# Three of eight token tiles through dense expert products, beside the gather of the other five

## The reference

```
xn = rms_norm(h, norm_mix)                       # keys and branches stages
merged = sum over 3 branches of sigmoid(gate_b) * (y_b @ w_proj_b)
h = h + merged @ w_out                           # merge
xt = rms_norm(h, norm_ffn)
q = (xt @ wq).reshape(T, 8, 2, 128);  s = einsum('thpc,hpkc->thpk', q, keys)
s1, i1 = top_k(s[:, :, 0], 16);  s2, i2 = top_k(s[:, :, 1], 16)
top_s, sel = top_k(all 256 sums s1 + s2, 16);  eid = i1 * 128 + i2 of the selected
gate = softmax(top_s)
act = gelu(u_tab[eid] . xt);  h = h + sum of gate * act * v_tab[eid]   # 8 heads x 16
h = h + sigmoid(rms_norm(h, norm_ple) @ ple_gate) * (p @ ple_proj)
```

## Time and profile before

| | |
|---|---|
| median of 3 runs | 4248.98 us (4239.84 to 4253.56) |
| profiled execution, its own time | 4245.94 us |
| its span | 4244.1 us, 36303 instructions |
| TensorE busy | 3058.3 us, 72% |
| VectorE busy | 2838.0 us, 67% |
| ScalarE busy | 1270.4 us, 30% |
| GpSimd busy | 1201.3 us, 28% |
| DMA | 1206.54 MB, mean 284 GB/s; 1073.81 MB of it by GpSimd's queue |
| mean granted TensorE clock | 0.845 |

### The profile page before, as it was taken

The page is one execution under the profiler, slowest core; times in us unless marked ns, Lnnn a source line. Parts: engine busy times, 40 slices in busy tenths (PEclk is TensorE's granted clock), DMA queues, the critical chain, the costliest instruction groups (busy, mean ns, idle before and its releaser), DMA issues.

```text
span 4244.1 us, 36303 instructions
## 1 busy us (share of the span) xinstructions
PE 3058.3 (72%) x7816; PEld 1457.8 (34%) x7816; DVE 2838.0 (67%) x5382; ACT 1270.4 (30%) x3456; POOL 1201.3 (28%) x1092
## 2 busy tenths in 40 slices
PE   8979998899999556665666656566667666566655
PEld 4535555444444323232232223223323233232321
DVE  3345555111111498889888888888888888888885
ACT  3223333010111133343333333333333333333322
POOL 0000000000000144444444444444443444444442
PEclk9989998899999778797787788778777877787877
DMA  4330010610110699999999999999999999999996
GB/s 169 115 112 32 30 41 28 240 42 27 40 42 27 264 411 395 414 398 403 381 377 401 398 375 405 384 381 407 390 409 368 409 394 377 406 394 397 410 403 275
DMA packets 192741, 1206.54 MB, mean 284 GB/s; under 512 B 21232, under 2 KB 27632, under 8 KB 60912
## 3 DMA queue, kind: packets, MB, share of 16 engines
q0 software_dynamic: 147456, 1073.81, 62.2%
q1 hardware_dynamic: 42864, 123.25, 8.0%
q10 hardware_dynamic: 2304, 8.39, 0.5%
HBM read 1173.91 MB, written 31.46 MB: 284 GB/s over the span
## 4 chain that ended last, share of the span: by engine, by line
DVE 27%; DMA 14%; issue 14%; PE 5%; ACT 3%; DVEq 1%; POOL 1%; ACTq 0%; POOLq 0%
DMA e_rows<-in_peer_uv,e_at 14%; DVE e_acc L1346 8%; DVE e_prod L1336 7%; PE e_acc L1110 2%; PE e_p_q L117 2%; DVE e_top_at L1298 2%; DVE e_best_at L1298 1%; DVE e_top L1297 1%; DVE e_best L1297 1%; DVE e_s L1300 1%; PE e_p_t L1124 1%; DVE e_hot L1324 1%; DVE e_expert L1325 1%; DVE e_cand L1300 1%; POOL e_rows L1030 1%
## 5 line engine op out<-in xcount | busy, mean ns | idle before, releaser
L1110 PE MATMUL e_acc<-e_rows,e_diag 128*128 128x512 f32 x2048 | 1318.8, 783 | 974.2 <-ACT e_diag L1247 973.8
L1030 POOL DMA_INDIRECT e_rows<-in_peer_uv,e_at x1024 | 1172.9, 1145 | 1556.6 <-DVE e_acc L1346 1216.4
L1336 DVE SCALAR_TENSOR_TENSOR e_prod<-e_rows,e_xn 128x1024 bf16<-128x1024 f32 x1024 | 1223.6, 1223 | 257.2 <-DMA e_rows<-in_peer_uv,e_at 166.0
L1110 PEld LDWEIGHTS e_acc<-e_rows,e_diag 128*128 128x128 f32 x2048 | 444.1, 236 | 1729.9 <-ACT e_diag L1247 1346.2
L1346 DVE SCALAR_TENSOR_TENSOR e_acc<-e_rows,e_wts,e_acc 128x1024 f32<-128x1024 f32 x504 | 647.8, 1285 | 56.3 <-ACT e_wts L1248 56.2
L1024 POOL CAST e_at<-e_expert 128x16 uint32 (+1 forms) x64 | 28.2, 441 | 1439.6 <-DVE e_expert L1325 1439.3
L1243 ACT ACTIVATE e_dots<-e_dots 128x2 f32<-128x2 f32 x512 | 104.1, 203 | 1017.3 <-DVE e_prod L1336 995.3
L117 PE MATMUL e_p_q<-e_wq,e_xnt 128*128 128x256 f32 (+1 forms) x1024 | 271.3, 425 | 25.5 <-ACT e_xnt L1177 19.0
L117 PE MATMUL m_p_g<-m_wg,m_xnt 128*128 128x512 f32 x640 | 281.2, 592 | 0.0
L117 PEld LDWEIGHTS e_p_q<-e_wq,e_xnt 128*128 128x128 f32 x1024 | 228.4, 224 | 110.6 <-issue 67.1
L937 DVE TENSOR_TENSOR m_part<-m_p_p,m_sg 128x512 f32<-128x512 f32 x32 | 22.4, 700 | 299.3 <-PE m_p_p L117 299.3
(11 more groups left out here) (250 smaller groups left out, 3073.8 us busy)
## 6 DMA issues: line engine op xcount, KB each, us to landing
e_rows<-in_peer_uv,e_at POOLq DMA_INDIRECT x1024, 9.0
m_wg<-in_w_gates SPq DMA_DIRECT2D x5, 2048.0 KB, 17.2
mix_w_branches<-in_w_branches_kept SPq DMA_DIRECT2D x8, 768.0 KB, 4.6
kept_yt<-b_yt SPq DMA_DIRECT2D x8, 768.0 KB, 3.6
m_yt<-kept_yt SPq DMA_DIRECT2D x8, 768.0 KB, 4.8
m_wp<-in_w_proj SPq DMA_DIRECT2D x6, 1024.0 KB, 16.3
e_wq<-in_peer_wq SPq DMA_DIRECT2D x1, 5120.0 KB, 24.9
k_x<-in_x SPq DMA_DIRECT2D x8, 512.0 KB, 5.5
```

The source lines that it names most:

```text
L1030: pool.indirect_dma_start(out=rows[:, n % SLOTS, :], out_offset=None, in_=A["peer_uv"], in_offset=bass.IndirectOffsetOnAxis(ap=at[:, b, n: ...
L1110: ins = pe.matmul(acc2[:, hs], diag[k % 2][:], rows[:, n % SLOTS, D + half * HB:D + (half + 1) * HB], start=first, stop=last)
L1336: dve.scalar_tensor_tensor(out=prod[n % 2][:], in0=rows[:, n % SLOTS, 0:D], scalar=1.0, in1=xn[:], op0=ALU.mult, op1=ALU.mult, accum_out=d ...
```

## The change

`merge_stage` and `experts_stage` become one `late_stage`, written out without loops in numbered slots by a planner (`Plan`). Tiles come in groups: 5, 6, 7, then 0, 1, then 2, 3, 4. Within a group each weight chunk of 1 MB (`CHUNK` = 2048 columns by 128 partitions) is loaded once into a ring of five (`RING`) and used by all the group's tiles; no weights are kept.

Tiles 5 to 7 (`DENSE`) gather nothing. All 16384 experts are computed for their 384 tokens: 32 blocks of 512 experts, each with four first products (`S`, eight matmuls 128x128 by 128x384, gelu on ScalarE, product with the gates on VectorE) and six second products (`V`, four matmuls of 512 columns, added to the sum by VectorE). The gates come from a DRAM tensor `g` of 16384 x 384 numbers: SP fills it with zeros in the keys stage (64 DMAs of 0.39 MB), and GpSimd scatters each chosen gate into it by indirect DMAs of 128 single numbers that add to what is there, 16 a head, 384 in all. Each head waits for the landing of the tile's last head. 192 of them are issued before the first gather, the other 192 two behind each gather of the first 48 slots.

The other five tiles are gathered, 640 gathers, in 320 slots of one pair each (`first` to `end`). Of four places VectorE now adds three and TensorE one (`on_tensor`); the sum `acc` lies in SBUF. The planner spreads the jobs of group 2, the dense blocks and the per-layer gate by their TensorE times evenly over these slots, behind the diagonal product of the slot before. Scores go over DRAM. Searches are done for 26 heads before the first pair, then one head in eight slots. The core of the diff (`sp` of the keys stage, the planner, and the programs of the slots):

```diff
+                for a in range(cleared.shape[2]):
+                    sp.dma_start(cleared[t][:, a, :], zeros[:]).then_inc(zeros_in, 16)
...
+GROUPS = ((5, 6, 7), (0, 1), (2, 3, 4))
...
+def on_tensor(n):
+    return n % 4 == 3
...
+            self.group(g)
+            if g == 1:
+                self.start = self.of["score", g, 3]
+        self.dense()
+        self.ple(DENSE + tuple(range(GATHER - 1)))
...
+                    for m in (2 * part, 2 * part + 1):
+                        self.add((i, m), "S", 5.3, pa=1, chunk=c, n_chunks=1, s=i, m=m)
...
+                    for d in range(len(DENSE)):
+                        self.add((i - 1, part, d), "V", 3.5, pb=1, chunk=c, n_chunks=1, s=i - 1, half=part, d=d)
...
+        self.first = slot + 3
+        rest = list(jobs)
+        us, budget = 0.0, sum(job.us for job in rest) / (PAIRS - 6)
...
+            slot = self.first + int(us / budget) + late
...
+            def load_chunk(n):
+                if n >= RING:
+                    before = plan.last_job[n - RING]
...
+                source, at = plan.chunks[n]
+                sp.dma_start(chunk(n), A[source][at]).then_inc(ring_in[n % RING], 16)
...
+                pool.wait_ge(chosen, q + 1)
+                pool.tensor_copy(at_dense[:, q, :], expert_of(q)).then_inc(dense_at_ready, 1)
...
+                wait(pool, gates_added[d], q // len(DENSE) * TOPK * 16)
...
+                pool.indirect_dma_start(out=X["g"], out_offset=bass.IndirectOffsetOnAxis(ap=at_dense[:, q, k:k + 1], axis=0),
+                                        in_=gates[:, q, k:k + 1], in_offset=None, compute_op=ALU.add).then_inc(gates_added[d], 16)
...
+            early = PH * len(DENSE) * TOPK - 8 * 24
...
+            for g in range(PAIRS):
+                row(2 * g)
+                for q, k in todo[done:done + SCATTERS_A_SLOT // 2]:
+                    scatter(q, k)
...
+            for s in range(plan.n_slots):
+                g = pair_of(s - 1)
+                if g is not None:
+                    for r in (2 * g, 2 * g + 1):
+                        if on_tensor(r % TOPK):
+                            weigh(r)
+                for job in plan.at[s]:
+                    programs[job.kind](job)
...
+                for job in plan.at[s - 1] if s else ():
+                    if job.kind in programs:
+                        programs[job.kind](job)
...
+                if pair_of(s) is not None:
+                    weights(pair_of(s))
...
+                for job in plan.at[s - 1] if s else ():
+                    if job.kind in programs:
+                        programs[job.kind](job)
+                g = pair_of(s - 1)
+                if g is not None:
+                    for r in (2 * g, 2 * g + 1):
+                        if not on_tensor(r % TOPK):
+                            weigh(r)
...
+                if pair_of(s) is not None:
+                    dot(2 * pair_of(s))
+                    dot(2 * pair_of(s) + 1)
+                for q, part in plan.parts[s]:
+                    (search_keys, search_pairs, choose)[part](q)
```

More of the change, by code:

```diff
@@ new lines, in weigh @@
+            def weigh(r):
+                c, n = divmod(r, TOPK)
+                pe.wait_ge(diag_ready, n_pe(r) + 1)
+                if r % NSEL < 4:
+                    wait(pe, h2_ready, r // NSEL)
+                first, last = r % NSEL < 4, r % NSEL >= NSEL - 4
+                for half in range(2):
+                    hs = slice(half * HB, (half + 1) * HB)
+                    ins = pe.matmul(acc2[:, hs], diag[n_pe(r) % 2][:], rows[:, r % SLOTS, D + half * HB:D + (half + 1) * HB], start=first, stop=last)
+                ins.then_inc(acc2_done, 1)
@@ new lines, in _ @@
+            qturn_of = {job.y: job for job in plan.jobs if job.kind == "qturn"}
+            programs = {"gate": sigmoid_gate, "turn": keep_merged, "xt": keep_normed, "query": keep_query, "qturn": keep_turned, "score": keep_scores,
+                        "S": activate, "hturn": keep_sum, "pgate": sigmoid_sum}
+            norms_at = [[] for _ in range(plan.n_slots)]
+            for g, group in enumerate(GROUPS):
+                for i in range(len(group)):
+                    norms_at[plan.of["out", g, 1, i].slot + 2].append((g, i))
@@ L1397, in _ @@
-            for r in range(LEAD):
-                order.turn()
-                search(r, 0)
-                search(r, 1)
-                pairs(r)
-                choose(r, part(r, 0, N))
-                reciprocal_sum(r)
-            tiles(dve, tile)
-            reciprocal_rms(T - 1)
-            output(T - 1)
-SPILLS = {"xnt": [T, P, DC * P], "v": [T, P, RW], "kt": [T, P, RW], "yt": [T, P, 3 * RW], "pp": [T, P, D], "h": [T, P, D], "xn": [T, P, D]}
+                to = expert_of(q)
+                ins = dve.tensor_reduce(to, hot[:].rearrange("p a k b -> p a (k b)"), AX.X, ALU.add)
@@ new lines, in finish @@
+            def finish(t):
+                dve.wait_ge(acc_done, n_dve((t + 1) * NSEL))
+                dve.wait_ge(acc2_done, n_pe((t + 1) * NSEL))
+                tt(acc[:, t % 2, :], acc[:, t % 2, :], acc2[:], ALU.add).then_inc(h2_ready, 1)
+                dve.wait_ge(h2_ready, t + 1)
+            programs = {"proj": merge, "out": add_input, "S": gate_block, "V": add_block, "hturn": reciprocal_rms, "pgate": output}
+            scales_at = [[] for _ in range(plan.n_slots)]
+            for g, group in enumerate(GROUPS):
+                for i in range(len(group)):
+                    scales_at[plan.of["out", g, 1, i].slot + 3].append((g, i))
```

1249 lines of the change are left out of this document (763 added, 486 removed).

## The result

The changed kernel takes 4346.47 us (median of four runs, 4342.12 to 4350.7), the one before 4250.49 us beside it: 1.0232 times as long, interval 1.0211 to 1.0253. It is 2.3% slower. Forecast were 3948 us; even the range, up to 4200, was missed. A difference of 0.3% is about what these measurements can tell.

A forecast was written before the change was run, and what follows sets the result against it. DMA was taken to bound the gather (65% of the span), TensorE the merge. Start of late stage 804.5, lead-in 600, gather 2505 and tail 36 made 3945.5 us; forecast 3948 us, range for 8 in 10 3740 to 4200.

The forecast's parts named there:

- The two-slot chain: Gather slots: dots, diagonal product, TensorE's jobs, VectorE's additions, updates go round in two slots; 7.6 us a slot, chance 0.57.
- The clock's term: Gather slots: 7.42 us of TensorE at a clock of 0.92 add 0.65 us to the two-slot round.
- the plain sums: Gather slots, each engine's work added up: DMA 7.1 us a slot, TensorE 6.5, VectorE 6.1.
- the three signs of being wrong: A block's 7.3 slots under 50 or over 62 us, first 48 slots over 600, or lead-in past 660.
- The scatters' issue: GpSimd: 0.94 + 0.30 us a scatter in the lead-in; 8.7 us for six issues in the first 48 slots, taken as 9.3.
- The rival of the scatters: First 48 slots: scatters at 2.7 us each in the DMA queue, 17.0 us a slot, 4318 us total; chance 0.13.
- below 1 us: DMA queue: cost of one adding scatter, bounds nothing to 2.7 us, hidden under GpSimd's 1.45 us an issue.
- The estimate of 131 us: DMA: what 192 scatters would add by the skill's 0.68 us for 4 KB; speaks against the edit.
- The per-layer gate: Last 24 gather slots, with the per-layer gate: 7.0 us each, 168 us.
- The keys stage: Zeros queued ahead of the rotary table delay it 3 us a tile, 25 us in all, bounds 0 and 65.
- The rivals of DMA and clock: Gather slots: DMA alone paces, 3719 us total, chance 0.13; TensorE stays at clock 0.80, 4135 us total, chance 0.15.

The follow-up runs named there:

- Experiment 4: Changed kernel with VectorE's products and additions of the dense blocks after the slot's dots instead of before its updates: 4053.08 us.
- experiment 1: Changed kernel without all 384 scatters and SP's waits for their landing (dense tiles' gates stay zero): 4134.48 us.
- experiment 2: Changed kernel with scatters that write instead of adding, so a later gate replaces an earlier one: 4163.61 us.
- Experiment 3: Changed kernel with the per-layer gate's product planned two slots behind its transposes: 4303.72 us.
- experiment 7: Changed kernel with all VectorE jobs behind the dots, the gate's ScalarE jobs behind the weights, and its product two slots behind its transposes: 3980.42 us.
- experiment 5: Changed kernel with each chunk of dense expert weights loaded only to a sixteenth, products unchanged: 4344.53 us.
- experiment 6: Changed kernel with VectorE's dense jobs after the dots and each chunk of dense expert weights loaded to a sixteenth: 4052.01 us.
- 12: experiment 7 with VectorE's dense gate products and additions left out for all but 32 columns: 3928.1 us.
- 8: experiment 7 with TensorE adding one row of eight instead of one of four, VectorE seven: 4024.25 us.

## Why the prediction was wrong, point by point

**The two-slot chain (step: "7.6 us a slot").** This is the step that failed most, 158 us. The mechanism was named rightly: the chain closes through VectorE's additions of TensorE's jobs. Its size was 8.28 instead of 7.6. I had summed pieces, each "ready" when its turn came, and taken 0.65 us for the clock and some for unevenness. The sum has no term for an engine that stands idle while its next instructions are ready: VectorE behind L1675 or L1683, with the updates and dots that free the ring and feed TensorE behind it. Experiment 4 prices the order at 1.25 us a slot, 291 us. I had read these lines of the diff, counted the additions, and never asked what stands behind them on the engine. The clock's term was about right: it gave 0.33 us a slot, and TensorE's busy time fell by 0.38 when the order was mended. Without that order the slots take 7.03, below my 7.6 and near the plain sums.

**The signs.** Of the three signs of being wrong that the prediction set, only one showed, and barely: the lead-in is past 660 us (664.6). A block's 7.3 slots took 60.4 us (over 62 was the sign) and the first 48 slots 539.7 (over 600). The losses lay inside these bounds and added up, and the per-layer gate had no bound at all.

**The scatters' issue (step: "6 x (1.145 + 0.30) = 8.7 us", and 1.24 us before the gather).** Mis-sized. I priced an adding scatter as a gather; it is 1.55 us and not 0.94. 192 x 1.85 = 355 us of GpSimd in place of 238 pushed the first dot 61 us out (experiment 1: the lead-in without them is 604 us, where 600 was forecast). In the 48 slots four scatters at 1.74 + 0.30 and two gathers at 1.17 + 0.30 make 11.1 of the 11.24 us, by the groups on GpSimd in the changed kernel from 1444 to 1984 us:

```profile
L1286 POOL DMA_INDIRECT kept_g<-l_gates,l_at_dense x190 | 330.0, 1737 | 57.7 <-issue 54.2 <-POOL l_at_dense L1277 3.2 <-DVE l_acc L1763 0.3
L1302 POOL DMA_INDIRECT l_rows<-in_peer_uv,l_at x100 | 117.0, 1170 | 30.3 <-issue 27.4 <-POOL l_at L1295 1.6 <-DVE l_acc L1763 1.2
```

With plain scatters the slots took 8.78 (experiment 2), the 8.7 of my sum: what it lacked is the addition. Together, lead-in and slots, 158 of the 396 us. The unknown of this resource was bounded for the DMA queue (0 to 2.7 us) and not for the engine that issues.

**The rival of the scatters.** It said slower, by the queue, from 15.6 us a slot on. The slots took 11.24 with the DMA 0.81 busy: the kernel is slower, but not by that rival's mechanism.

What a scatter costs the DMA can be read in the lead-in, where GpSimd's queue carries little else. First row: changed kernel, 779 to 1444 us, 194 adding scatters. Second: experiment 2, 774 to 1378 us, 198 plain ones (packets, MB, share of the 16 engines):

```profile
q0 software_dynamic: 27950, 1.16, 11.4%
```

```profile
q0 software_dynamic: 6398, 1.54, 1.3%
```

That is 144 packets and 0.39 us of the 16 engines for an adding scatter, 32 packets and about 0.04 us for a plain one. My "below 1 us" held, and the DMA had room for it (0.49 busy in the lead-in, 0.81 in the 48 slots). So what was dear is the addition, on GpSimd. Whether its 0.59 us go into the larger number of packets or into something else was not tested.
The Trainium skill, "DMA: Bandwidth & Descriptors", Specifications, has pieces under 512 bytes read and written back. The estimate of 131 us for 192 scatters, from the 0.68 us for 4 KB in its section Bandwidth, compares with some 75 us for adding scatters here and 8 for plain ones of the same size; in the 48 slots GpSimd was full in both cases, and the DMA was not.

**The per-layer gate (step: "24 at 7.0").** Wrong, 119 us. Seven waits of 16 to 29 us, 166 in all, were not seen, as I added these jobs up and did not follow the chain inside a slot. Experiment 3 takes back 48 us of it, experiment 7 another 28.

**The keys stage (25 us).** Mis-sized at its end, not in its kind. The table's wait is there, 69.6 us over seven tiles (waits of the changed kernel from 40 to 260 us):

```profile
DVE k_ra L129 <- DMA k_tab<-in_rotary: 69.6, 7, 10.6
```

Ahead of the table's load stand, in its time line, the eight issues of zeros:

```profile
207.16 6.48 SPq L251 DMA_DIRECT2D kept_g<-k_zeros  x8
```

The zeros took 6.5 us to issue, where I had put some 4. The table's wait stands in place of another, which the kernel before has in the same window and the changed one has not:

```profile
DVE k_ra L128 <- PE k_p_k L117: 45.5, 7, 7.5
```

So VectorE lost 24 us there net, 3.4 a tile, close to the forecast's 3. But only part of it reached the end: the last product of the branches starts at 769.31 us, 10.5 later than before (758.79). Where the rest was made good was not followed. And the late stage then waits only 8.87 us for its input, where the merge stage had waited 16.20 for its weights, so that its first product comes at 779.29 against 776.10.

**The rivals of DMA and clock.** The DMA was 0.90 busy in the dense slots and not the bound, as experiment 5 shows, and experiment 6 for the mended order. The clock was 0.93 in the dense slots and 0.81 and 0.74 in the two stretches where TensorE idles. It followed the idle time: without scatters it is 0.91 in those 48 slots, with the other order 0.98 in the dense ones.
Experiments 4 and 7 reach what was forecast for the whole (3948) within 1 to 3%, and partly by luck: their dense slots are faster than I said and their scatters dearer.

**Break-even.** The change loses 96 us net. The order of VectorE's instructions is worth 290, the addition in the scatters 180, the per-layer gate's one slot 40 to 75. Either of the first two put right turns the sign (4053.08; 4163.61 with the sums left out; before 4250.49).

**Left open.** What holds the slots of experiment 7 at 7.02 us is shown in part. TensorE is nearest to it: in the 1591 us shown it is busy 1523.5 us, and its largest wait adds 60.2:

```profile
PE l_acc L1442 <- ACT l_diag L1598: 60.2, 43, 2.9
```

Its work of 6.7 us a slot is a floor, and the wait hangs on VectorE's dots (0.87 busy). With VectorE thinned (12) that wait fell to 35.8 us in 1541; with more work on VectorE (8) it rose to 147.5 in 1591. So the two share the slot, and no run took work from TensorE without giving some to VectorE. Bytes were excluded only with the order of experiment 4 (6).

## What to carry to other kernels

In an order written out by hand, put first on each engine what releases others (here the updates that free the ring, the dots that feed TensorE) and last what waits for a third engine; then a late result delays only itself. Sum each engine's work for a first look, but price a slot by walking through it instruction by instruction, asking of each wait what ready work stands behind it. An operation that no row shows needs bounds on the engine that issues it as well as on the resource that it uses.

## What the runs showed of the hardware

- An indirect DMA of 128 single floats holds GpSimd 0.96 us when it writes and 1.55 us when it adds, with nothing to wait for; a gather of 128 rows of 8 KB took 0.94. In the DMA queue the first is 32 packets and about 0.04 us of the 16 engines, the second 144 packets and 0.39 us.
- A DMA share of 1.00 at 405 GB/s was no bound: with 330 GB/s and 0.89 the same slots took the same time (experiments 4 and 6).
- A gather's issue was 1145 ns in the mean before and 1634 ns in the dense slots of the changed kernel, where the sum that VectorE updates lies in SBUF and no longer in PSUM. This is the row of the changed kernel on GpSimd between 2100 and 4000 us:

```profile
L1302 POOL DMA_INDIRECT l_rows<-in_peer_uv,l_at x460 | 751.6, 1634 | 1148.0 <-DVE l_acc L1763 1057.4 <-issue 63.5 <-PE l_acc L1438 27.1
```

The time lines say what the long issues ran beside. In the kernel before, an issue inside an update (sum in PSUM), and one beside the two dots of the earlier trace rows:

```profile
2332.76 1.28 DVE L1346 SCALAR_TENSOR_TENSOR e_acc<-e_rows,e_wts,e_acc 128x1024 f32<-128x1024 f32 x1
2332.80 0.94 POOL L1030 DMA_INDIRECT e_rows<-in_peer_uv,e_at  x1 [0.30 <-issue]
...
2346.72 1.82 POOL L1030 DMA_INDIRECT e_rows<-in_peer_uv,e_at  x1 [0.30 <-issue]
```

From 2000 to 3000 us of that kernel the 47 issues that overlap an update, and a dot for 0.05 us at most, all take 0.93 to 0.95 us, and the 166 that overlap dots, which read two tiles in SBUF, for over 0.3 us take 1.35 in the mean. From 2200 to 3200 us of the changed kernel each of the 165 issues of 1.6 us and more overlaps a dot. No issue there overlaps an update alone, so what the sum's place adds is not isolated.
The Trainium skill, "SBUF — State Buffer", SBUF: two separate sides, has GpSimd and a VectorE instruction with two SBUF inputs exclude each other. The time lines agree for the dots, and the 0.49 us by which the mean rose is within the 1.2 us estimated from it. It cost nothing in the dense slots, as GpSimd had over 1000 us to spare; in the 48 slots with scatters, where GpSimd is full, an adding scatter took 1.74 us in the mean and not 1.55, so there it may have cost something.
